# Retention's masked scores times values: three passes over operands split into a high and a low part, in place of float32 products

## The reference, cut to what matters

```python
q, k, v, g = split(h @ w_in)             # per head: q, k 256 wide, v, g 512 wide
q = rotate(q); k = rotate(k) * 256 ** -0.5
scores = (q @ k.T) * decay_mask          # causal decay
out = scores @ v                         # (chunked in the reference; the same sum)
out = out * rsqrt(mean(out * out) + eps) * silu(g)
return out @ w_out
```

## Time and profile before

| | |
|---|---|
| median of 3 runs | 1026.45 us (1024.38 to 1027.12) |
| the profiled execution: its time | 1024.93 us |
| its span in the trace | 1023.1 us |
| TensorE (PE) busy | 1014.5 us, 99% of the span |
| VectorE (DVE) busy | 788.6 us, 77% |
| ScalarE (ACT) busy | 497.7 us, 49% |
| GpSimd (POOL) busy | 98.3 us, 10% |
| granted TensorE clock | 1.000 of full speed over the span |

### The profile page before, as it was taken

How to read it: one execution, slowest core, us unless ns; L and a number is a source line. 1 busy time by engine, 2 the same in 40 slices (tenths; PEclk the granted TensorE clock), 3 DMA queues, 4 the chain that set the end, 5 groups by cost and what they waited for, 6 DMA issues and landing times.

```text
span 1023.1 us, 15913 instructions
## 1 busy us (share of the span) xinstructions
PE 1014.5 (99%) x5922; PEld 888.5 (87%) x5922; DVE 788.6 (77%) x902; ACT 497.7 (49%) x536; POOL 98.3 (10%) x91
## 2 busy tenths in 40 slices
PE   8999999999999999999999999999999999999998
PEld 7888888888888888888888888888887898888888
DVE  6987876788788778877767797788668977887743
ACT  7455434544444354454444454564447854554432
POOL 0000013101100152000013100000330031000000
PEclk9999999999999999999999999999999999999999
DMA  8665356652553444654455645534662245554461
GB/s 324 260 210 200 129 179 207 259 211 85 215 195 103 185 165 165 211 199 170 152 182 197 244 165 204 201 129 154 207 235 101 87 165 197 192 184 167 150 194 65
DMA packets 32293, 185.28 MB, mean 181 GB/s; under 512 B 3840, under 2 KB 6400, under 8 KB 16128
## 3 DMA queue, kind: packets, MB, share of 16 engines
q1 hardware_dynamic: 32112, 184.77, 51.1%
q10 hardware_dynamic: 144, 0.03, 0.0%
HBM read 183.73 MB, written 1.05 MB: 181 GB/s over the span
## 4 chain that ended last, share of the span: by engine, by line
PE 95%; DVE 2%; ACT 1%; DMA 1%; SPq 1%; issue 0%; POOL 0%; POOLq 0%; DVEq 0%; ACTq 0%
PE ps L1136 95%; DMA stage<-w_in_dram 1%; DVE w_lo L638 1%; SPq L285 0%; SPq L283 0%; ACT w_hi L327 0%; PE ps L1415 0%; ACT x_sq L611 0%; POOL y_sq L1122 0%; DVE x_sq L1054 0%; DVE sm L969 0%; DVE hs L860 0%; PE ps L1382 0%; ACT w_hi L608 0%; ACT y_sq L484 0%
## 5 line engine op out<-in xcount | busy, mean ns | idle before, releaser
L1136 PE MATMUL ps<-h,w_hi 128*128 128x512 f32 x1664 | 582.3, 395 | 1.5 <-DVE h L674 1.2
L1136 PE MATMUL ps<-h,w_lo 128*128 128x256 f32 x1664 | 466.2, 280 | 0.0
L638 DVE TENSOR_TENSOR w_lo<-stage,w_hi 128x2048 fp32r<-128x2048 f32 (+1 forms) x190 | 397.1, 2099 | 28.8 <-ACT w_hi L327 28.5
L1136 PEld LDWEIGHTS ps<-h,w_hi 128*128 128x128 f32 x1664 | 312.2, 188 | 71.8 <-DVE w_lo L1070 1.0
L327 ACT ACTIVATE w_hi<-stage 128x2048 fp32r<-128x2048 f32 (+1 forms) x190 | 326.7, 1727 | 9.5 <-PE ps L1136 8.1
L1136 PEld LDWEIGHTS ps<-h,w_lo 128*128 128x128 f32 x1664 | 315.0, 189 | 0.3
L1136 PE MATMUL ps<-act_t,w_hi 128*128 128x512 f32 (+1 forms) x726 | 245.7, 387 | 0.0
L1136 PE MATMUL ps<-act_t,w_lo 128*128 128x256 f32 x704 | 197.3, 280 | 0.0
L1136 PEld LDWEIGHTS ps<-act_t,w_hi 128*128 128x128 f32 x726 | 134.7, 188 | 29.3
L359 ACT ACTIVATE tmp<-ps 128x1024 f32<-128x1024 f32 x44 | 45.1, 1026 | 183.2 <-PE ps L1136 181.7
L1136 PEld LDWEIGHTS ps<-act_t,w_lo 128*128 128x128 f32 x704 | 133.2, 189 | 0.0
(11 more groups left out here) (154 smaller groups left out, 747.8 us busy)
## 6 DMA issues: line engine op xcount, KB each, us to landing
stage<-w_in_dram SPq DMA_DIRECT2D x85, 1024.0 KB, 4.8
stage<-w_out_dram SPq DMA_DIRECT2D x64, 704.0 KB, 4.1
stage<-w_ret_dram SPq DMA_DIRECT2D x24, 1024.0 KB, 4.8
stage<-w_ret_out_dram SPq DMA_DIRECT2D x8, 1024.0 KB, 4.8
stage<-w_q_dram SPq DMA_DIRECT2D x4, 1024.0 KB, 4.9
stage<-w_o_dram SPq DMA_DIRECT2D x4, 1024.0 KB, 4.8
stage<-w_in_dram SPq DMA_DIRECT2D x8, 256.0 KB, 5.8
x<-x_t_dram SPq DMA_DIRECT2D x8, 128.0 KB, 5.9
```

Of the source, the lines that this page charges most:

```text
L638: nc.vector.tensor_tensor(w_lo[:, s, 0:n], stage[:, s, 0:n], w_hi[:, s, 0:n].bitcast(F32), ALU.subtract).then_inc(lo_ready, 1)
L1136: return nc.tensor.matmul(out_, w, x_, start=start, stop=stop)
```

## The change

The copy of the values by ScalarE now writes `v_hi` as fp32r; VectorE forms `v_lo` = values - `v_hi` from PSUM (128 x 1024) in one instruction between `split(u + 6)` and `split(u + 7)`. After the mask products ScalarE rounds the masked scores to `s_hi` (128 x 384), in its program between `lo_half(2)` and `split(u + 8)`, and VectorE forms `s_lo` in place of `s_mask`, between the mask products and its `split(u + 8)`. On TensorE each of the 8 float32 products of a head becomes three fp32r ones; `pair(u + 5)` waits for `v_split` (the low part of the values) instead of the copy, and the product for `masked_lo` instead of `masked`.

```diff
-    v_nat = at("v_nat", [P, 2, DV], F32, big + 36864)
+    v_hi = at("v_hi", [P, 2, DV], F32R, big + 36864)
...
+    s_lo = at("s_lo", [P, 384], F32R, aux + 8192)
+    s_hi = at("s_hi", [P, 384], F32R, aux + 14848)
...
+    v_lo = at("tmp_r", [P, 2, 1024], F32R, misc + 8192)[:, :, 512:1024]
...
+    v_split, masked_hi, masked_lo = sem("v_split"), sem("masked_hi"), sem("masked_lo")
...
                 act.wait_ge(used, u + 4)
-                nc.scalar.activation(v_nat[:], ps[:, 0:2, :], ACT.Copy).then_inc(v_copied, 1)
+                nc.scalar.activation(v_hi[:], ps[:, 0:2, :], ACT.Copy).then_inc(v_copied, 1)
                 split(u + 7)
                 lo_half(2)
+
+                act.wait_ge(masked, c + 1)
+                nc.scalar.activation(s_hi[:], s_mask[:], ACT.Copy).then_inc(masked_hi, 1)
                 split(u + 8)
                 silu(2)
                 lo_half(3)
...
                 split(u + 6)
+
+                dve.wait_ge(v_copied, c + 1)
+                nc.vector.tensor_tensor(v_lo, ps[:, 0:2, :], v_hi[:].bitcast(F32), ALU.subtract).then_inc(v_split, 1)
                 split(u + 7)
                 add_halves(2)
                 scale_gate(2)
...
                 nc.vector.tensor_tensor(s_mask[:, T:T + P], ps[:, 4, T:T + P], decay_s[:, c, 0:P],
                                         ALU.mult).then_inc(masked, 1)
+                dve.wait_ge(masked_hi, c + 1)
+                nc.vector.tensor_tensor(s_lo[:], s_mask[:], s_hi[:].bitcast(F32),
+                                        ALU.subtract).then_inc(masked_lo, 1)
                 split(u + 8)
                 add_halves(3)
                 scale_gate(3)
...
-                pe.wait_ge(v_copied, c + 1)
+                pe.wait_ge(v_split, c + 1)
                 pair(u + 5, 0, i)
 
-                pe.wait_ge(masked, c + 1)
+                pe.wait_ge(masked_lo, c + 1)
                 pe.wait_ge(y_done, c + 1)
                 for e in range(4):
                     o = ps[:, 5 + e // 2, T * (e % 2):T * (e % 2 + 1)]
-                    matmul(o, v_nat[:, 0, e * P:(e + 1) * P], s_mask[:, 0:T], True, False)
-                    last = matmul(o[:, P:T], v_nat[:, 1, e * P:(e + 1) * P], s_mask[:, T:T + P], False, True)
+                    for kb, out_, cols in ((0, o, slice(0, T)), (1, o[:, P:T], slice(T, T + P))):
+                        hi, lo = (v[:, kb, e * P:(e + 1) * P] for v in (v_hi, v_lo))
+                        matmul(out_, hi, s_hi[:, cols], kb == 0, False)
+                        matmul(out_, hi, s_lo[:, cols], False, False)
+                        last = matmul(out_, lo, s_hi[:, cols], False, kb == 1)
                 last.then_inc(pv_done, 1)
```

## The result

| | before | changed |
|---|---|---|
| median | 1027.07 us (10 runs, 1024.38 to 1030.74) | 1030.09 us (10 runs, 1028.12 to 1033.23) |
| ratio | | 1.0034, 95% interval 1.0021 to 1.0047 |
| span of the profiled execution | 1023.1 us | 1031.4 us |

The changed kernel is slower by 3.0 us, 0.34%. So the comparison goes by distances within the stage.

A forecast was written before the change was run, and what follows sets the result against it. TensorE, busy 99% of the span, was taken as the bound. Delays of 0.62 + 0.84 + 0.84 + 1.50 = 3.8 us over four heads, on the median of 1026.45, gave 1030.2 us; range 1027.5 to 1033.0.

The forecast's parts named there:

- part 1: TensorE's products: 24 fp32r ones cost 2.76 to 3.96 us a head instead of 2.53; lower end taken.
- The lower end of the bounds: 128-column fp32r products on TensorE: 12 take 1.32 us, paced by weight loads 0.11 us apart; group 2.76 us.
- The first rival: TensorE's short fp32r matmul costs 0.21 us like the float32 one: 5.8 us more in all, 1032.2; chance 0.27.
- The estimate by the Trainium skill's figure: TensorE's products: some 81 ns per 128-column matmul, so 2.41 us a group, 0.12 us less than now.
- part 2: VectorE's subtraction takes 1.22 us, delays everything behind it by 1.14; pair(u + 5) keeps 0.36 us in hand, no cost.
- part 3: ScalarE's wait for mask products delays both weight splits and add_halves(3); the next head starts 0.84 us later (0.65 to 0.95).
- The last term: Behind head 3, y_sq and GpSimd's sum come late, so head_sum(4) starts 1.50 us later.
- The rival on the other side: Not slower: add_halves(3) ends before 267.1 in head 1, ScalarE's wait is covered; 0.9 us remain, 1027.4; chance 0.16.

The follow-up runs named there:

- e1: The changed kernel run again unaltered, against the kernel before: 1030.20 us, ratio 1.0038.
- e10: The changed kernel run a third time unaltered, against the kernel before: 1028.51 us, ratio 1.0019.
- e4: The 24 fp32r products without the preparation (low parts left out, result not the reference's), against the kernel before: 1027.58 us, ratio 1.0004.
- e8: e2 with VectorE's subtraction for the values behind split(u + 7) instead of ahead of it: 1034.69 us, 1.0075 to the kernel before.
- e2: The changed kernel with ScalarE's split(u + 8) ahead of s_hi instead of behind it: 1027.20 us, 1.0010 to the kernel before.
- e3: The changed kernel with all preparation and waits, but the 8 plain float32 products as before: 1030.28 us, 1.0038 to the kernel before.
- e7: e3 without VectorE's subtraction for the values: 1026.80 us, 0.9999 to the kernel before.

## Why the prediction was right, by its own steps

**The result.** 1030.2 was predicted, 1030.09 measured; the sum was +3.8 us on the path, the stage grew by 3.66 to 3.92 in three profiles. That the two totals agree to 0.1 us is partly luck: the kernel before has a median of 1027.07 over ten runs and not the 1026.45 that the sum started from, and the medians moved by 3.0 us (3.4 in e1, 1.7 in e10), less than the stage in its profiles. Why less isn't shown; single executions of one kernel differ by more than this gap.

**The products (part 1)** were expected at 2.76 us a head and took 2.70 (e4). The lower end of the bounds was the right one. Three 128-column fp32r matmuls start 0.05 and 0.12 us apart in the rows of head 1 (270.25, 270.30, 270.42), and the wide one behind such a group is followed at 0.17 (269.84 to 270.01) instead of 0.12; with that, a group of three costs 0.33 us, 0.11 each, as far apart as the weight loads of the earlier trace rows. The first rival, a short fp32r matmul at 0.21 us, fell. The estimate by the Trainium skill's figure ("TensorE: Matmul & The Clock Gate", section "Back-to-back issue gap"), 2.41 us, was too low for the whole group; of the two readings the one by the row of weight loads was nearer.

**VectorE's subtraction for the values (part 2)** took the 1.22 us of its row and was on time for `pair(u + 5)`: in the changed kernel no wait of TensorE is put down to it, and e8 shows what it costs where the cover is gone. From the end of the last mask product to the first product it is 267.82 - 265.78 = 2.04 us, where it was 264.69 - 261.51 = 3.18: the 1.14 by which all behind it was to come later.

**ScalarE's wait (part 3)**, the main step, held link by link: ScalarE idle 4.14 us (4.2 expected), `s_hi` 0.53 us (0.49), VectorE idle 1.25 us (1.3), and from the end of the last mask product to the start of `add_halves(3)` 270.38 - 265.78 = 4.60 us (267.23 - 262.65 = 4.58). That it decides is shown by e2 (the wait moved, the cost gone) and e3 (the cost there without the products). TensorE began 0.24 us after `add_halves(3)` ended (271.06 to 271.30), where 0.14 was taken.

**By head**, from `q_cs` to the first matmul of each next head, and last to `head_sum(4)`. Two of these rows of TensorE aren't shown above:

```profile
232.67 0.49 PE L1149 MATMUL ps<-h,w_hi 128*128 128x512 f32 x1
...
309.81 0.49 PE L1149 MATMUL ps<-h,w_hi 128*128 128x512 f32 x1 [0.50 <-DVE tmp L884]
```

| | before | changed | longer | predicted |
|---|---|---|---|---|
| `q_cs` to head 1 | 229.55 - 206.30 = 23.25 | 232.67 - 208.80 = 23.87 | 0.62 | 0.62 |
| head 1 | 267.22 - 229.55 = 37.67 | 271.30 - 232.67 = 38.63 | 0.96 | 0.84 |
| head 2 | 304.89 - 267.22 = 37.67 | 309.81 - 271.30 = 38.51 | 0.84 | 0.84 |
| head 3, to `head_sum(4)` | 347.05 - 304.89 = 42.16 | 353.21 - 309.81 = 43.40 | 1.24 | 1.50 |

The last term was 0.26 too large, and what was off isn't the wait: `y_sq` started 1.54 us later (349.50 - 309.81 = 39.69, where it was 343.04 - 304.89 = 38.15), as against 1.50. But the prediction carried GpSimd's first sum over at the 1.96 us of the earlier trace rows, and it took 1.69:

```profile
348.84 2.28 DVE L645 TENSOR_TENSOR w_lo<-stage,w_hi 128x2048 fp32r<-128x2048 f32 x1
350.58 1.69 POOL L1135 TENSOR_TENSOR y_sq<-y_sq 128x512 f32<-128x512 f32 x1 [35.94 <-ACT y_sq L491]
```

Before, VectorE's weight split at this place was this one:

```profile
342.66 2.29 DVE L638 TENSOR_TENSOR w_lo<-stage,w_hi 128x2048 fp32r<-128x2048 f32 x1 [0.38 <-ACT w_hi L327]
```

It overlaps with GpSimd's sum (from 344.14) for 0.81 us, in the changed kernel for 0.54. Less the overlap, the sum takes 1.15 us in both. In part for the same reason the idle time before `head_sum(4)` grew to 0.46 us and not to the 0.9 that had been predicted. Part of the good total is therefore luck: head 1 was 0.12 more than predicted, head 3 0.26 less.

**The rival on the other side** said that the wait would be covered if the chain on VectorE ended 0.8 us earlier. e7, without the subtraction that had been put at 1.14 us, did just that: +0.13 us. The rival named the subtraction as part of what would have to be cheaper; that each of the two additions costs next to nothing without the other it didn't say. It means that either of them, put into the old program alone, would have looked free.

## What to carry to other kernels

Where engines work through their programs in order, ask of a new wait not what it waits for but what stands behind it: here a weight split that had nothing to do with the scores, then VectorE, then TensorE. Put the instruction that waits behind the ones that are ready (e2: one line, 2.8 of the stage's 3.7 us). Before more passes of a cheaper type replace fewer of a dearer one, count the distance between starts for each width: here three fp32r passes of 128 columns cost 0.33 us for a float32 product of about 0.21, 0.11 each, the distance from one weight load to the next, while three of 256 columns cost 0.36 for one of about 0.42 (both float32 prices by 1.65 ns a column).

## What had not been expected of the hardware

Identical instructions of TensorE ran at two paces, with the granted clock at 1.00 in both. The same stretch of the first feed-forward, timeline of the changed kernel's first profile, from which eight pairs of matmuls take 102.67 - 99.85 = 2.82 us:

```profile
99.85 0.40 PE L1149 MATMUL ps<-h,w_hi 128*128 128x512 f32 x1
...
102.67 0.40 PE L1149 MATMUL ps<-h,w_hi 128*128 128x512 f32 x1
```

and of the kernel before, 102.53 - 99.76 = 2.77 us:

```profile
99.76 0.39 PE L1136 MATMUL ps<-h,w_hi 128*128 128x512 f32 x1
...
102.53 0.39 PE L1136 MATMUL ps<-h,w_hi 128*128 128x512 f32 x1
```

Such stretches come and go between executions of one kernel: the changed kernel's first profile begins the retention stage 2.5 us later than the kernel before (208.80 against 206.30 at `q_cs`), its second 0.1 us earlier (206.16). Within the retention stage one pattern repeats: behind float32 products or an idle time of TensorE a pair takes 0.3465 us (e3, head 2: twelve pairs from 269.10 to 273.26), behind fp32r products without a wait 0.353 (e2, head 2: nine pairs from 270.78 to 273.96). With 16 pairs to a weight unit that is 0.1 us a unit, against the products' own 0.17 a head, so it can't be neglected where tenths matter. No run was made to find the cause; it stays open.

GpSimd's first sum of squares makes no headway while VectorE's weight split runs. In all 12 profiles, four heads each, the sum lasts between 1.69 and 1.97 us and begins while a split is running; less the part that overlaps with the split it takes 1.14 to 1.17 us every time. Four of them from head 3: before 1.96 with 0.81 of overlap, changed 1.69 with 0.54, e2 1.76 with 0.61, e7 1.69 with 0.55. So a delay of the sum moves it out from under the split and gets part of itself back, which is why e7 cost 0.13 us and not the expected 0.4. That it is the split that holds it up is read from these overlaps; no run moved one of the two alone.
